# One step of a hybrid decoder with a mixture of experts: the put matrix of an expert is transposed ahead of the last quarter of its down product

## What is computed

```python
logits = xf @ w_router + b_router
top_val, top_idx = lax.top_k(logits, 4)
top_w = softmax(top_val)
# for each expert, for its tokens:
gate = minimum(xb @ w_gate[e] + b_gate[e], 7)
up = clip(xb @ w_up[e] + b_up[e], -7, 7)
out = ((up + 1) * gate * sigmoid(1.702 * gate)) @ w_down[e] + b_down[e]
# y[token] += top_w * out[token], then x + g2 * y and a last RMSNorm
```

## Time and profile before

| | |
|---|---|
| median of 3 runs | 1842.5 us (1839.04 to 1848.12) |
| the profiled execution's own time | 1845.33 us |
| its span | 1843.6 us |
| mean granted clock of the tensor engine in it | 0.94 |
| tensor engine busy | 1628.4 us (88%) |
| VectorE busy | 762.5 us (41%) |
| ScalarE busy | 422.8 us (23%) |
| loads of expert weights | 3 x 128 of 1 MB |

### The profile page before, as it was taken

The page is one execution under the profiler, slowest core; times in us unless marked ns, Lnnn a source line. Parts: engine busy times, 40 slices in busy tenths (PEclk is TensorE's granted clock), DMA queues, the critical chain, the costliest instruction groups (busy, mean ns, idle before and its releaser), DMA issues. The chain is left out here.

```text
span 1843.6 us, 24041 instructions
## 1 busy us (share of the span) xinstructions
PE 1628.4 (88%) x8449; PEld 873.5 (47%) x8450; DVE 762.5 (41%) x1519; ACT 422.8 (23%) x806; POOL 126.9 (7%) x208
## 2 busy tenths in 40 slices
PE   6997898899978999878898898999898989999994
PEld 3775584686855676563233233333333333333332
DVE  2355332344252001283634635422626446345374
ACT  3235113120011200123312313211313223132132
POOL 0211120211210410000000000000000000000000
PEclk9899998999589999988999999999999999999997
DMA  9362108113017534306999999996999999999993
GB/s 312 139 220 77 68 1 315 50 47 103 0 48 238 191 137 149 126 1 275 425 424 397 426 426 416 425 365 248 425 386 426 424 389 425 426 394 426 403 426 129
DMA packets 115089, 494.61 MB, mean 268 GB/s; under 512 B 9947, under 2 KB 27548, under 8 KB 65831
## 3 DMA queue, kind: packets, MB, share of 16 engines
q1 hardware_dynamic: 113050, 491.21, 67.1%
q10 hardware_dynamic: 1984, 2.64, 0.5%
HBM read 487.39 MB, written 6.43 MB: 268 GB/s over the span
## 5 line engine op out<-in xcount | busy, mean ns | idle before, releaser
L763 PE MATMUL ps_mix<-hT,ring 128*128 128x320 f32 x896 | 263.8, 451 | 21.4 <-DVE ring L1235 10.6
L763 PEld LDWEIGHTS ps_mix<-hT,ring 128*128 128x128 f32 x896 | 175.5, 199 | 101.4 <-issue 16.4
L1906 PE MATMUL ps_moe<-ring,hT_moe 128*64 128x512 f32 x672 | 159.6, 635 | 2.6 <-ACT hT_moe L1849 2.6
L1906 PE MATMUL ps_moe<-ext,xg 128*64 128x512 f32 x672 | 147.5, 594 | 1.8 <-issue 0.9
L1906 PE MATMUL ps_moe<-ring,xg 128*64 128x512 f32 x672 | 147.7, 594 | 1.3 <-DMA ring<-in_w_up 1.3
L2092 DVE TENSOR_SCALAR hid<-ps_moe 128x256 f32<-128x256 f32 (+1 forms) x96 | 48.8, 508 | 152.8 <-ACT hid L1841 111.1
L1906 PEld LDWEIGHTS ps_moe<-ring,hT_moe 128*64 128x64 f32 x672 | 55.0, 147 | 100.2 <-issue 99.9
L2078 DVE TENSOR_SCALAR gate<-ps_moe 128x1024 f32<-128x1024 f32 x32 | 39.2, 1225 | 151.2 <-ACT hid L1836 101.3
L2064 DVE TENSOR_TENSOR work<-work,ps_moe 128x640 f32<-128x640 f32 x128 | 99.2, 815 | 1.4 <-PE ps_moe L1922 0.3
L1906 PEld LDWEIGHTS ps_moe<-ext,xg 128*64 128x64 f32 x672 | 47.6, 137 | 96.6 <-issue 92.7
L1906 PEld LDWEIGHTS ps_moe<-ring,xg 128*64 128x64 f32 x672 | 46.8, 137 | 93.2 <-issue 89.3
(11 more groups left out here) (410 smaller groups left out, 2232.7 us busy)
## 6 DMA issues: line engine op xcount, KB each, us to landing
ext<-in_w_gate SPq DMA_DIRECT2D x128, 1024.0 KB, 16.3
ring<-in_w_up SPq DMA_DIRECT2D x128, 1024.0 KB, 16.5
ring<-in_w_down SPq DMA_DIRECT2D x128, 1024.0 KB, 13.6
ring<-in_w_in SPq DMA_DIRECT2D x18, 2048.0 KB, 8.2
ring<-in_w_ada SPq DMA_DIRECT2D x12, 2048.0 KB, 9.7
ext<-in_state_gdn_rec SPq DMA_DIRECT2D x8, 512.0 KB, 7.1
out_rec_sample<-ext SPq DMA_DIRECT2D x8, 512.0 KB, 6.1
ring<-in_w_branch_b SPq DMA_DIRECT2D x2, 2048.0 KB, 10.3
```

The source lines that it names most:

```text
L763: last = nc.tensor.matmul(out, ring[:, place(i), k, P * j:P * j + P], rhs[:, k, :], start=k == 0, stop=k == NC - 1)
L1906: ends = [nc.tensor.matmul(ps[MID * a:MID * a + MID, bank + blk, :], lhs(blk, c), w[:, k, HALF * a:HALF * a + HALF], start=c == 0 and not ...
```

## The change

In `down`, `turn_put` and the wait for `comb_s` are moved from behind the product into `ready`, for the last quarter. There they stand behind the wait for the last piece of weights and ahead of the last quarter's matmuls. All three forms do this. Nothing is changed on the other engines.

```diff
                         def ready(q):
                             if q < 2:
                                 pe.wait_ge(hT_s, 3 * i + (3 if blocks == 2 else q + 1))
+                            if q == 3:
+                                if not first_of_pass:
+                                    pe.wait_ge(comb_s, 4 * i)
+                                turn_put(i, blocks)
                         if blocks == 0:
                             strip_product(i, 2, 4, lambda c: hT[:, 0, c % 4, STRIP * (c // 4):STRIP * (c // 4) + STRIP], ready)
                         else:
                             product(i, 2, 4, blocks, lambda blk, c: hT[:, blk, c % 4, MID * (c // 4):MID * (c // 4) + MID], ready)
-                        if not first_of_pass:
-                            pe.wait_ge(comb_s, 4 * i)
-                        turn_put(i, blocks)
                         if blocks == 0:
                             join_strips(i, 3, 4)
```

## The result

| | before | changed |
|---|---|---|
| median | 1844.07 us (4 runs, 1839.04 to 1848.12) | 1888.12 us (4 runs, 1887.42 to 1891.48) |
| ratio, 95% interval | | 1.0246 [1.0226, 1.0265] |
| profiled execution: own time, span | 1845.33, 1843.6 us | 1891.48, 1889.8 us |
| mean granted clock in it | 0.940 | 0.932 |

The changed kernel is 44 us slower, where 25.5 us were forecast. The spans differ by 46.2 us, and the stretch from the first expert's gate product to the end of the last down product by 46.4 us (968.2 against 1014.6), so all of it lies in the expert loop. In the changed kernel the lines behind the diff have numbers one higher: L2064 is L2065, L2055 is L2056.

What follows compares the result with a forecast made beforehand. The tensor engine was taken as the bound; 23.9 + 2.7 + 4.3 = 30.9 us, less 5.4 us of landing waits, gave 25.5 us on 1842.5, so 1868.0 us. Its own range was 1860 to 1877, for 8 in 10 1851 to 1881.

Steps and rivals of the forecast that it cites:

- the distance behind the fold: Narrow expert: next gate product stays 1.3 us behind the fold, so both come 1.84 us later, in 13 experts.
- the three experts with 0.89: Three other narrow experts behind the fourth, where VectorE's sums are done in time: 0.89 us each, together 2.7 us.
- The tensor engine is therefore the bound: Expert loop from about 1060 us to the last expert: a tensor engine delay goes on to the end.
- The landing waits give back their 2.8 + 2.6 = 5.4 us: Tensor engine's waits for down and up weights, two places each, absorb 5.4 us of the added 30.9 us.
- The moved wait of 1.17 us: Ahead of a narrow expert's last quarter, the wait for VectorE's sums (L2064) stands uncovered, 1.17 us in 13 experts.
- Delays in the first three experts vanish in the landing waits of the fourth: Start of the expert loop: delays there add nothing to the forecast time.
- 0.62 us later: Behind a wide expert, put copies and pairs come 0.62 us later, in 7 places before a narrow expert: 4.3 us.
- the rival with the clock lost in all 13 narrow experts: Rival: new idles lower the narrow experts' clock, 1.45 us each, 18.9 us more, 1887 us (three experts: 1872); chance 0.14.
- No change: Rival: the DMA queue hides the delay and the tensor engine only waits less; time 1843, chance 0.09.
- half: Rival: the fold's copy or weight loads are covered and only the wait costs; 1852 to 1855, chance 0.10.
- faster: Rival: put copies come early and the pairs' waits of 11.7 us over 7 places shrink; time 1831, chance 0.05.

Runs made afterwards that it cites:

- experiment 10: Kernel before, with the move for middle and wide experts alone, their put matrix copied ahead of the sums and made first by VectorE; 1842.64 us, 1.0000.
- experiment 11: Kernel before with experiment 10's edits plus 2 x 4 unused matmuls in wide experts' waits for the hidden rows; 1831.41 us, 0.9928.
- experiment 3: Changed kernel with the transposes put into free PSUM banks 2 and 3, so no wait for `comb_s`; 1875.37 us, 1.0176 against before.
- experiment 6: Only the wait for `comb_s` moved ahead of the last quarter, transposes left behind the product; 1859.65 us, 1.0079 against before.
- experiment 7: Changed kernel with the transposes made a second time, unused, behind a narrow expert's last quarter; 1891.98 us, 1.0263 against before.
- experiment 5: Changed kernel, but the first expert of the pass keeps its transposes behind the down product; 1887.92 us, 1.0247 against before.
- experiment 2: Changed kernel with the move made in middle and wide experts alone, narrow ones keeping the old place; 1855.39 us, 1.0056 against before.
- experiment 4: Changed kernel, but ScalarE copies the put matrix (L1821) ahead of the down product's sums (L1817); 1873.69 us, 1.0161 against before.
- experiment 8: Changed kernel with 8 unused matmuls ahead of the pairs' wait behind a wide expert; 1878.72 us, 1.0197 against before.
- experiment 1: Changed kernel with the move made in narrow experts alone, middle and wide ones keeping the old place; 1877.65 us, 1.0187 against before.
- experiment 12: Changed kernel with 8 unused matmuls ahead of pairs behind wide experts and 2 x 4 in wide experts' hidden-row waits; 1875.28 us, 1.0176 against before.

## Why the prediction was wrong

The direction and the order of events were right, the size was not: 44 us against 25.5, and 1888 us is above the 1851 to 1881 given for 8 in 10. Step by step, with the forecast's own words. The step that failed first is the distance behind the fold; then come the three experts with 0.89, the entry, and the clock on the pairs.

- *"The tensor engine is therefore the bound"*: right. Delays of 2.15 us in narrow experts went on to the end. *"The landing waits give back their 2.8 + 2.6 = 5.4 us"*: right, 6.7 us found, and no product waits for a landing afterwards. This holds for delays; for gains of the engine, experiments 10 and 11 found nothing more below some 10 us.
- *The moved wait of 1.17 us*: right, 1.13 to 1.17 us each, shown from both sides by experiments 3 and 6.
- *"The fold thus comes at 2.38 - 1.36 + 0.82 = 1.84 us later, and the next gate product, 1.3 us behind the fold in both"*: this step failed. I read 1.3 us between two array rows as a fixed distance. The fixed distance is the one from ScalarE's copy, 1.87 us in both kernels, whatever the array does in it (experiment 7). The 0.54 us that an earlier fold should have given back aren't there; 0.3 us came back elsewhere, at the pairs, where I had written that it gives nothing back. 2.15 instead of 1.84.
- *"3 x 0.89"*: failed too. In these three experts a landing wait or a low clock had given VectorE's sums time to be done, which I had not asked. With these gone, 15 of 16 wait for L2065. This and the last point are 36.5 - 26.6 = 10 us.
- *"Delays in the first three experts vanish in the landing waits of the fourth"*: failed in part, +4.4 us. The landing waits took the ordinary delays, but not all of an idle of 6 us at the loop's entry that the trace of before doesn't have. Its price is from the profile alone, since experiment 5 couldn't resolve it.
- *Wide expert, "0.62 us later"*: the wait grew by 0.51 us, so its size was right. What failed is what hangs on it: the low clock, which I priced at 1.45 us each and gave 0.14, I put into the narrow experts, where the idles are shorter and the clock mostly stayed. It came on the pairs behind a wide expert, 6 more times of 7, some 9 to 10 us (experiments 2, 4, 8). The price per place was right and the place wrong. That the rival with the clock lost in all 13 narrow experts gives 1887 us, next to the 1888 measured, is luck: its 18.9 us stand where the runs have 9 to 10 us at the pairs, and the rest is the 10 us and the 4.4 us above. The rule that I cited from the Trainium skill, TensorE: Matmul & The Clock Gate, section A second HAM failure mode, that small idles between groups of matmuls throttle the clock again, is borne out here by a stretch of 1.2 GHz in all 7 places (the pairs shown above took 2.44 us for 1.44), and by experiment 8, which fills the idle and has the 1.44 us back.
- *The rivals.* No change, half, and faster are refuted by the time. The first of them leaned on DMA shares up to 1.00; with these, a delay of the tensor engine was still passed on. What the forecast held against the faster case, ScalarE's order, was right: with the order changed (experiment 4) the pairs' wait halved.

What stays open: the price of the entry. In the profiles the stretch ahead of the fifth expert is 4.2 to 4.7 us longer than before in the changed kernel and in experiments 1, 4, 7 and 8. In experiment 3 it is as long as before, although the idle stands there too (8.3 us from the down product to the next gate product): its first gate product is 1.2 us shorter, and the down products of the first three experts, without the wait, 1.1 to 1.2 us each. In experiment 12 it is 10.4 us longer, because the second expert has one more such idle, ahead of its down product (9.6 us from the up product's end, where the changed kernel has 4.5). The idle at the entry stands in all seven kernels in which the first expert's transposes are ahead of its last quarter (7.35 to 8.33 us from down product to gate product), and in none of the seven others (2.65 to 3.05 us). It isn't the lost cover: in experiment 7 the transposes behind the product are back, and 7.8 us stand there. Why the moved transposes bring it isn't known.

## What to carry to other kernels

A step moved ahead of a product takes its wait along: price the wait by when its releaser is done, and ask what had stood in the free time at the old place. Between two waits measure from the event that releases, not from the array's rows in between, since the way from that event may be what takes the time. Behind every wait that grows, look at the durations of the next matmuls: an idle of 2.2 us cost 1.5 us more through the clock, and a few matmuls with unused results in the wait keep the clock, which here made the kernel before 0.6% (medians) to 0.75% (ratio) faster. Count the low clock over the whole loop, as it can leave one place and come up in another (experiments 4 and 10).

## What the runs showed of the hardware

- The stretches of 1.2 GHz hang on short idles. The wide expert's waits for the hidden rows, under 1 us each, brought them in 7 of 8 down products; with 8 small matmuls in these waits the clock stayed at 2.4 GHz there, and the time at 1.2 GHz from the fifth expert on fell from 37.5 to 3.4 us. The idle alone doesn't decide: the one down product of before at full clock has the same idles ahead of it (0.93, 0.28 and 0.82 us) as one with a stretch of 1.2 GHz (0.94, 0.28 and 0.82 us). The same idle of 1.1 us ahead of the last quarter in narrow experts mostly brought none.
- From the release of a narrow expert's fold to the next expert's first matmul it takes 1.87 us if this is narrow, 1.74 if it is middle and 1.49 if it is wide, whether the array has the fold alone in that time or six transposes as well.
- The idles put down to "issue" in the first experts stand beside fetches of instructions. The DMA view of single microseconds of the changed kernel has one such packet from 870 to 871 us, within the idle that ends at 872.97, and none from 856 to 870:

```profile
q8 instruction: 1, 0.02, 6.4%
```

  In before one lands between 862 and 863 us, ahead of the gate product at 865.41 without such an idle. In experiment 12 one starts between 869 and 870, and the gate product starts at 872.22 behind 5.47 us of idle; the next idle of 4.28 us ends at 890.50, behind a packet at 888 to 889. The Trainium skill, Runtime: NRT & Kernel Launch, section Instruction fetch mechanics, says that a taken branch to code outside what has been fetched makes the engine wait for a fetch. The traces agree in place and order, in 3 idles that each end 2 to 3 us behind the start of a packet; that a fetch is their cause wasn't tried. Against it stands that the view doesn't say for which engine a packet is, and that three more, at 876, 883 and 889 us of the changed kernel, have no such idle behind them.
